# Two transformer blocks on one core: V as weights in two column groups, and scores from high and low parts, in three attentions

## The chip, the cores and the metric

The kernel runs on one core of a Trainium2 chip. The metric is the device time of one execution in microseconds. The work is issued by hand to the engines: TensorE (PE in the profile; its weight loads are PEld), VectorE (DVE), ScalarE (ACT), GpSimd (POOL) and SyncE (SP), which issues the DMA transfers. Each engine works through its own queue in order; semaphores order them among each other.

## The reference

Two blocks of two layers each, on 512 rows of x and 256 rows of context, width 1024, everything float32. The first block has a layer with two dense attentions side by side, then one with a windowed attention beside a short convolution:

```python
q, k, v, gate = heads(h @ w_in)            # norm, gain and rotation on q and k
kk, vv = concat(k_context, k), concat(v_context, v)
p = softmax(q @ kk.T * d ** -0.5)          # MLA: 8 heads, d = 96; GQA: 8 heads on 2 key heads, d = 64
o = p @ vv                                 # value width 64
mix = concat(o_mla, o_gqa) * silu(gate)
x = x + gate_of_modulation * (mix @ w_out) # the context rows too, with context keys alone
# second layer: 8 heads on 2 key heads, d = 64, a band of 3 blocks of 128 keys and the 256 context keys,
# softmax with one more logit per head (the sink)
```

The second block has three more attentions with values 128 wide, which the change leaves alone.

## The kernel before

Rows lie in tiles of 128: four of x (XT), two of context (CT). A projection is a chain of products whose float32 operands are split in a high part, rounded to fp32r, and a low part (the rest); three passes high x high, high x low and low x high give the product (L839 to L841). The five attentions share one function per engine, `attention(name)`: TensorE at L943, ScalarE at L1191, VectorE at L1514. The first three are "gqa", "mla" and "win". Their values are 64 wide; the heads are 64, 96 and 64.

A **unit** j is one head and one tile of 128 queries (`units_of`, L417). gqa and mla have 48 units: per head four x tiles with 768 keys (six blocks of 128) and two context tiles with 256 keys (two blocks), in the order 0, 4, 1, 5, 2, 3. win has 32: per head the tiles 0 to 3 with four, five, five and four blocks. All engines loop over j, and LAG = 1 (L429) staggers the steps. In iteration j they do, each in this order:

- TensorE: scores of unit j into a pair of PSUM banks (L994 and L995 for gqa, L997 for the others); turns (`prep`, L954) of q or k of the next head, from rows to columns, into bank 7; turns of the probabilities of unit j-1 (L1020) into banks 4 and 5; the product of the probabilities with V of unit j-2 (L1032) into bank 6, the turned probabilities as 128 x 128 weights and V as the 64 moving columns; then, in some iterations, a product of a modulation unit (L898, eight small products with 32 weight columns and 128 moving columns, in four column groups), its turn (L907), or a gate spread over all rows (L916).
- ScalarE: copies of the turned q or k (L1206; for gqa the high part, L1200); the exponential of unit j (L1226); the second part of the turned probabilities of unit j-1 (L1240); the copy of a modulation row (L1256).
- VectorE: a finished modulation column (L1463); the row maximum of unit j, as a minimum of negated scores (L1551, with a mask L1553; in win a second, tiny minimum with the sink, L1556); the low part of q or k, for gqa (L1525, L1529); the first part of the turned probabilities of unit j-1 (L1569); the reciprocal of the row sum and the final scaling of unit j-2 out of bank 6 (L1580, L1597), called "mixed". In gqa the steps of mla's norms follow at the end of the iteration (`mla_norms`, L1665), and in win those of the convolution.

The order around bank 6 is written out by hand: a PSUM bank notes who reads it last, and who writes it next waits for that. The product with V of unit i waits in this way for the final scaling of unit i-1:

```python
                        bank_free(6)                                   # the reader noted last
                        for n_, b in enumerate(bl):
                            mm = eng.matmul(psum[:, 6, 0:dv], prT[...], v_rows(name, h, b), ...)
                        mm.then_inc(*to("product_v", (name, i)))
                        reader[6] = ("mixed", (name, i))
```

`STACKED` (L506) names the attentions whose scores are formed from high and low parts stacked along the contraction: the 64 rows of q high lie over those of q low, and two passes against k high over k high and k low over k low give the product. Before, this is gqa alone; mla and win take their scores in full float32 from 96 and 64 rows (L997). The DMA loads are issued by SyncE in one queue: constants, modulation weights, then the weights of every stage in order, three buffers deep.

## Time and profile before

| | |
|---|---|
| Median of 3 runs | 1721.77 us (1720.62 to 1725.77) |
| The profiled execution | 1723.44 us, span 1721.6 us |
| TensorE busy | 1624.8 us (94% of the span) |
| TensorE weight loads | 1342.5 us (78%), beside the products |
| VectorE busy | 899.1 us (52%) |
| ScalarE busy | 647.5 us (38%) |
| GpSimd busy | 566.9 us (33%) |
| Mean granted TensorE clock | 0.971 of full speed |

The span is the time from the first to the last instruction. Busy time is the time in which an engine had an instruction under way; the ends of matmuls are modelled. The three attentions of the change lie at 246 to 401 us (gqa), 401 to 549 us (mla) and 792 to 892 us (win). A row of the timeline can merge several instructions of one form (the number behind x); a product in float32 counts twice there, one in fp32r and a turn once.

### The profile page before, as it was taken

The page shows a single profiled execution, that of the slowest core. Times are in us where ns is not written, and L with a number is a line of the kernel's source. Part 1 is how long each engine was busy: PE and PEld are TensorE (multiplying, and loading weights), DVE is VectorE, ACT ScalarE, POOL GpSimd, SP SyncE. Part 2 cuts the span into 40 slices and gives each one's busy share as a digit, 9 for nine tenths or more (in the row PEclk, how much of TensorE's full clock was granted, in tenths as well). Part 3 has the DMA queues.
Part 4 walks back from the last instruction along what each step waited for, and adds up shares of the span by engine and source line. Part 5 has one row for each costly group of instructions (what it writes and reads, how often), then busy time and mean ns, then how long its engine had stood idle before and what let it go on. Part 6 is the DMA issues. An engine that isn't in the chain of part 4 may idle for free.

```text
span 1721.6 us, 24787 instructions
## 1 busy us (share of the span) xinstructions
PE 1624.8 (94%) x9120; PEld 1342.5 (78%) x9120; DVE 899.1 (52%) x2120; ACT 647.5 (38%) x1320; POOL 566.9 (33%) x333
## 2 busy tenths in 40 slices
PE   4999889899999979999999999989999999999998
PEld 1788878797887858887888789956578778887787
DVE  2655737665554244924752688036531279916422
ACT  3322354354454323334542433344333343336322
POOL 1222231860001333446505344410424534431134
PEclk9999989899999989999999999969999999999999
DMA  8321212231013112331003232300112222220222
GB/s 326 83 73 46 62 50 87 71 90 50 26 38 111 62 31 80 93 97 57 1 1 101 86 98 83 90 0 1 50 49 86 95 86 98 98 74 1 80 92 86
DMA packets 93158, 124.40 MB, mean 72 GB/s; under 512 B 10288, under 2 KB 52208, under 8 KB 92016
## 3 DMA queue, kind: packets, MB, share of 16 engines
q1 hardware_dynamic: 93040, 122.82, 22.5%
q8 instruction: 75, 1.23, 0.3%
q14 instruction: 43, 0.35, 0.1%
HBM read 120.70 MB, written 2.10 MB: 71 GB/s over the span
## 4 chain that ended last, share of the span: by engine, by line
PE 86%; DVE 7%; ACT 3%; issue 2%; DMA 1%; POOL 1%; SPq 0%; DVEq 0%; ACTq 0%; POOLq 0%
PE psum L839 18%; PE psum L841 18%; PE psum L840 18%; PE psum L1032 10%; PE psum L997 8%; PE psum L1020 5%; PE psum L809 3%; PE psum L954 3%; DMA mod_w<-mod_w_in 1%; PE psum L994 1%; PE psum L898 1%; PE psum L999 1%; PE psum L995 1%; ACT rz L1188 1%; DVE row_rstd L1346 0%
## 5 line engine op out<-in xcount | busy, mean ns | idle before, releaser
L1757 POOL TENSOR_TENSOR wlo<-wraw,whi 128x1024 fp32r<-128x1024 f32 (+4 forms) x172 | 399.7, 2325 | 979.1 <-ACT whi L1083 979.0
L1083 ACT ACTIVATE whi<-wraw 128x1024 fp32r<-128x1024 f32 (+4 forms) x172 | 174.7, 1019 | 483.3 <-PE psum L841 483.3
L839 PE MATMUL psum<-whi,h2h 128*128 128x512 f32 (+2 forms) x800 | 309.3, 387 | 7.1 <-ACT buf L1132 5.9
L841 PE MATMUL psum<-whi,h2l 128*128 128x512 f32 (+2 forms) x800 | 305.8, 382 | 0.0
L840 PE MATMUL psum<-wlo,h2h 128*128 128x512 f32 (+2 forms) x800 | 305.5, 382 | 0.0
L839 PE MATMUL psum<-whi,hTh 128*128 128x512 f32 (+2 forms) x512 | 196.9, 385 | 9.5 <-DVE hTl L1454 7.3
L1226 ACT ACTIVATE pr<-psum,nmax 128x512 f32<-128x512 f32 (+1 forms) x208 | 137.9, 663 | 170.9 <-DVE nmax L1551 88.3
L841 PE MATMUL psum<-whi,hTl 128*128 128x512 f32 (+2 forms) x512 | 192.0, 375 | 0.0
L840 PE MATMUL psum<-wlo,hTh 128*128 128x512 f32 (+2 forms) x512 | 192.0, 375 | 0.0
L839 PEld LDWEIGHTS psum<-whi,h2h 128*128 128x128 f32 x800 | 150.7, 188 | 33.4 <-issue 8.0
L997 PE MATMUL psum<-kT,qT 64*128 64x256 f32 (+5 forms) x480 | 164.6, 452 | 7.1 <-DVE qT L1536 4.3
L841 PEld LDWEIGHTS psum<-whi,h2l 128*128 128x128 f32 x800 | 150.6, 188 | 26.6
L840 PEld LDWEIGHTS psum<-wlo,h2h 128*128 128x128 f32 x800 | 150.7, 188 | 25.3
L1020 PE MATMUL psum<-ident,pr 128*128 128x128 f32 x792 | 130.6, 286 | 9.2 <-ACT pr L1226 7.2
L1020 PEld LDWEIGHTS psum<-ident,pr 128*128 128x128 f32 x792 | 94.8, 146 | 34.8 <-ACT pr L1226 18.6
L839 PEld LDWEIGHTS psum<-whi,hTh 128*128 128x128 f32 x512 | 98.0, 191 | 25.3 <-issue 9.7
L841 PEld LDWEIGHTS psum<-whi,hTl 128*128 128x128 f32 x512 | 97.9, 191 | 17.0
L840 PEld LDWEIGHTS psum<-wlo,hTh 128*128 128x128 f32 x512 | 98.2, 192 | 15.2
L1551 DVE TENSOR_REDUCE nmax<-psum 128x1 f32<-128x768 f32 x96 | 74.9, 780 | 65.9 <-PE psum L997 41.4
L997 PEld LDWEIGHTS psum<-kT,qT 64*128 64x128 f32 (+2 forms) x480 | 79.9, 193 | 35.7 <-issue 19.0
L1569 DVE COPY prT<-psum 128x256 f32<-128x256 f32 (+1 forms) x208 | 90.6, 435 | 23.3 <-PE psum L1020 21.1
L1032 PE MATMUL psum<-gq,prT 128*128 128x64 f32 x736 | 93.7, 274 | 1.1 <-DVE rz L1597 1.1
(253 smaller groups left out, 2459.8 us busy)
## 6 DMA issues: line engine op xcount, KB each, us to landing
wraw<-mod_w_in SPq DMA_DIRECT2D x32, 512.0 KB, 3.8
wraw<-w_in_odd_in SPq DMA_DIRECT2D x32, 512.0 KB, 3.4
wraw<-cd_w_in_in SPq DMA_DIRECT2D x24, 512.0 KB, 3.6
wraw<-w_in_even_in SPq DMA_DIRECT2D x20, 512.0 KB, 3.9
mod_w<-mod_w_in SPq DMA_DIRECT2D x8, 1024.0 KB, 17.8
wraw<-ab_w_in_in SPq DMA_DIRECT2D x16, 512.0 KB, 3.6
wraw<-w_ple_gate_in SPq DMA_DIRECT2D x16, 512.0 KB, 3.9
wraw<-ab_w_out_in SPq DMA_DIRECT2D x8, 512.0 KB, 3.6
```

The lines of the kernel that those rows point to most:

```text
L809: mm = eng.transpose(psum[:, b, n_ * P:(n_ + 1) * P], turn[name]["rows"](t, k), ident[:, :])
L839: eng.matmul(dst, a[0], ww[0], start=first, stop=False)
L840: eng.matmul(dst, a[0], ww[1], start=False, stop=False)
L841: mm = eng.matmul(dst, a[1], ww[0], start=False, stop=last_)
L997: mm = eng.matmul(dst, q_, ks[0:dk, a:b], start=True, stop=name != "fox")
L1020: mm = eng.transpose(psum[:, bk, (b - b0) * P:(b - b0 + 1) * P], pr[:, i % 2, b * P:(b + 1) * P], ident[:, :])
L1032: mm = eng.matmul(psum[:, 6, 0:dv], prT[:, i % 2, n_ * P:(n_ + 1) * P], v_rows(name, h, b), start=n_ == 0, stop=n_ == len(bl) - 1)
L1083: eng.activation(whi[:, s, :, 0:w], wraw[:, u["id"] % RAW, :, 0:w], ACT.Copy).then_inc(*to("split_hi", u["id"]))
L1226: eng.activation(pr[:, j % 2, 0:w], psum_flat[:, s0 * 512:s0 * 512 + w], ACT.Exp, bias=nmax[:, j % 4:j % 4 + 1], scale=-1.0, accum_out=rsu ...
L1551: eng.tensor_reduce(m, sc, AX.X, ALU.min).then_inc(*(label or note("nmax", (name, j))))
L1569: eng.tensor_copy(prT[:, i % 2, 0:nb * P], psum[:, 4, 0:nb * P]).then_inc(*note("probs_a", (name, i)))
L1757: eng.tensor_tensor(wlo[:, s, :, 0:w], wraw[:, u["id"] % RAW, :, 0:w], f32(whi[:, s, :, 0:w]), ALU.subtract)\
```

## The change

For gqa, mla and win ("HALVED") the product with V changes sides: V (128 keys x 64) is the weights and the turned probabilities (128 keys x 128 queries) are the moving columns. The even blocks of keys go to the columns 0 to 63 of the array and so to PSUM partitions 0 to 63 of bank 6, the odd blocks to 64 to 127. ScalarE copies this 128 x 128 result to the tile o2, and one more product with o2 as weights and a constant of two stacked 64 x 64 identities as moving operand adds both halves and turns the result back, again into bank 6. On TensorE it stands in the iteration after the product with V, behind the scores and the turns of q and k. VectorE's final scaling waits for it and moves to the next iteration as well; each loop has one iteration more.

The scores of win are stacked as gqa's were. Those of mla ("PARTED", 96 rows don't stack) are formed in three fp32r passes: q high with k high, q high with k low, q low with k high. The high parts are copied out by ScalarE and the low parts computed by VectorE, now for all three. In win the separate minimum with the sink becomes the start value of the masked minimum. The constant is loaded behind `sel`, and some small tiles change place.

```diff
+    out["halves"] = np.concatenate([np.eye(64), np.eye(64)]).astype(np.float32)
...
-        STACKED = ("gqa",)
+        STACKED, PARTED = ("gqa", "win"), ("mla",)
+        ROUNDED = STACKED + PARTED
+        HALVED = ("gqa", "mla", "win")
...
         def parts_of(name, p_):
-            key, _, _, tiles, dst, _ = p_
+            key, _, _, tiles, dst, d = p_
+            if name in PARTED:
+                lo = (qTl if key[0] == "q" else kTl)[0:d, key[1] % 2, tiles[0] * P:(tiles[-1] + 1) * P]
+                return [dst], [lo]
...
+            load(halves[:, :], io["k_halves"], "load_sel", 1)
...
     (TensorE, attention)
-                for j in range(n_units + lag + 1):
+                for j in range(n_units + lag + 1 + int(name in HALVED)):
...
                             if name in STACKED:
                                 eng.matmul(dst, q_, ks[:, a:b], start=True, stop=False)
                                 mm = eng.matmul(dst, q_, kl[:, a:b], start=False, stop=True)
+                            elif name in PARTED:
+                                eng.matmul(dst, q_, ks[0:dk, a:b], start=True, stop=False)
+                                eng.matmul(dst, q_, kTl[0:dk, h % 2, a:b], start=False, stop=False)
+                                mm = eng.matmul(dst, qTl[0:dk, h % 2, t * P:(t + 1) * P], ks[0:dk, a:b], start=False, stop=True)
...
+                    if name in HALVED and lag + 1 < j:
+                        i = j - lag - 2
+                        eng.wait_ge(*at("o2_copied", (name, i)))
+                        eng.matmul(psum[:, 6, 0:dv], o2[:, i % 2, :], halves[:, :], start=True, stop=True)\
+                           .then_inc(*to("joined", (name, i)))
+                        reader[6] = ("mixed", (name, i))
...
                         bank_free(6)
                         for n_, b in enumerate(bl):
+                            if name in HALVED:
+                                c0 = 64 * (n_ % 2)
+                                mm = eng.matmul(psum[c0:c0 + 64, 6, 0:P], v_rows(name, h, b), prT[:, i % 2, n_ * P:(n_ + 1) * P],
+                                                start=n_ < 2, stop=n_ >= len(bl) - 2)
+                                continue
                             mm = eng.matmul(psum[:, 6, 0:dv], prT[:, i % 2, n_ * P:(n_ + 1) * P], v_rows(name, h, b),
                                             start=n_ == 0, stop=n_ == len(bl) - 1)
                         mm.then_inc(*to("product_v", (name, i)))
-                        reader[6] = ("mixed", (name, i))
+                        reader[6] = ("o2_copied" if name in HALVED else "mixed", (name, i))
...
     (ScalarE, attention, after the second copy of turned probabilities)
+                    if name in HALVED and lag < j:
+                        i = j - lag - 1
+                        eng.wait_ge(*at("product_v", (name, i)))
+                        eng.activation(o2[:, i % 2, :], psum[:, 6, 0:P], ACT.Copy).then_inc(*to("o2_copied", (name, i)))
...
     (VectorE, attention)
-                for j in range(len(units) + lag + 1):
+                later = int(name in HALVED)
+                for j in range(len(units) + lag + 1 + later):
...
-                            eng.tensor_tensor_reduce(sc, sc, bias, 1.0, 3.0e38, ALU.add, ALU.min, m).then_inc(*(label or note("nmax", (name, j))))
-                        if name == "win":
-                            after_last()
-                            eng.tensor_tensor(m, m, nsink[:, h:h + 1], ALU.min).then_inc(*note("nmax", (name, j)))
+                            most = nsink[:, h:h + 1] if name == "win" else 3.0e38
+                            eng.tensor_tensor_reduce(sc, sc, bias, 1.0, most, ALU.add, ALU.min, m).then_inc(*note("nmax", (name, j)))
...
-                    for p_ in preps.get(j, []) if name in STACKED else ():
+                    for p_ in preps.get(j, []) if name in ROUNDED else ():
                         low(p_)
...
-                    if lag < j:
-                        i = j - lag - 1
+                    if lag + later < j:
+                        i = j - lag - 1 - later
...
-                        eng.wait_ge(*at("product_v", (name, i)))
+                        eng.wait_ge(*at("joined" if later else "product_v", (name, i)))
```

## Rows read from the trace of the kernel before

**Rows 1.** The page, chain that ended last, by engine
```profile
PE 86%; DVE 7%; ACT 3%; issue 2%; DMA 1%; POOL 1%; SPq 0%; DVEq 0%; ACTq 0%; POOLq 0%
```

**Rows 2.** Busy by stretch (us): PE, PEld, DVE, ACT, POOL, clock, DMA, GB/s
```profile
246.50:400.90 154.40, 142.70 (x1316) 127.96 (x1316) 108.19 (x270) 66.84 (x170) 76.77 (x83) 0.93 0.29 83
401.00:549.00 148.00, 145.49 (x1104) 121.27 (x1104) 78.39 (x203) 72.75 (x174) 1.67 (x1) 1.00 0.16 51
792.00:892.00 100.00, 96.97 (x658) 83.00 (x658) 74.49 (x230) 53.98 (x147) 48.18 (x34) 1.00 0.03 12
```

**Rows 3.** Chain of waits: the same step of successive heads, gqa, then win
```profile
363.14 1.29 PE psum L1032 x12
...
379.31 1.29 PE psum L1032 x12
...
853.24 1.06 PE psum L1032 x10
...
864.68 1.06 PE psum L1032 x10
```

**Rows 4.** Timeline, mla: start, length in us, instruction, [idle before, releaser]
```profile
470.63 1.51 PE L997 MATMUL psum<-kT,qT 96*128 96x512 f32 x4
...
471.98 0.82 PE L1020 MATMUL psum<-ident,pr 128*128 128x128 f32 x6
...
472.18 0.96 DVE L1551 TENSOR_REDUCE nmax<-psum 128x1 f32<-128x768 f32 x1 [0.99 <-PE psum L997]
...
472.63 0.56 PE L1032 MATMUL psum<-cq,prT 128*128 128x64 f32 x4
...
473.05 0.55 DVE L1569 COPY prT<-psum 128x384 f32<-128x384 f32 x1
...
473.70 0.28 DVE L1597 SCALAR_TENSOR_TENSOR rz<-psum,rinv,rz 128x64 f32<-128x64 f32 x1
...
475.46 1.45 PE L1032 MATMUL psum<-cq,prT 128*128 128x64 f32 x12
...
476.84 0.64 PE L898 MATMUL psum<-wraw,silu_pad 128*32 128x128 f32 x16
...
477.42 0.70 PE L997 MATMUL psum<-kT,qT 96*128 96x256 f32 x2
```

**Rows 5.** Timeline, gqa, a low part, then a short and a long unit
```profile
363.14 0.68 DVE L1525 TENSOR_TENSOR qTs<-psum,qTs 64x512 fp32r<-64x512 f32 x1 [0.24 <-ACT qTs L1200]
...
370.80 0.38 PE L994 MATMUL psum<-kTs,qTs 128*128 128x256 f32 x1
...
371.34 0.42 DVE L1551 TENSOR_REDUCE nmax<-psum 128x1 f32<-128x256 f32 x1 [0.65 <-PE psum L995]
...
375.35 0.50 PE L994 MATMUL psum<-kTs,qTs 128*128 128x512 f32 x1
...
376.35 0.96 DVE L1551 TENSOR_REDUCE nmax<-psum 128x1 f32<-128x768 f32 x1 [1.12 <-PE psum L995]
```

**Rows 6.** Timeline, win
```profile
848.28 0.42 DVE L1569 COPY prT<-psum 128x256 f32<-128x256 f32 x1
...
848.60 1.35 PE L997 MATMUL psum<-kT,qT 64*128 64x256 f32 x6
...
849.01 0.28 DVE L1597 SCALAR_TENSOR_TENSOR rz<-psum,rinv,rz 128x64 f32<-128x64 f32 x1
...
849.88 0.77 PE L1020 MATMUL psum<-ident,pr 128*128 128x128 f32 x5
...
849.98 0.83 DVE L1553 CUSTOM_DVE_ANT_0 psum<-psum,bias_window 128x640 f32<-128x640 f32 x1 [0.69 <-PE psum L997]
```

**Rows 7.** Busy by stretch as in rows 2, two stretches of gqa
```profile
260.00:264.00 4.00, 2.45 (x21) 2.17 (x20) 3.65 (x8) 1.37 (x3) 1.83 (x2) 1.00 0.41 121
336.00:340.00 4.00, 4.00 (x19) 3.81 (x19) 1.76 (x5) 0.99 (x2) 3.84 (x3) 0.50 0.02 4
```

More of the change, by code:

```diff
@@ L148, in build @@
         ident = sb("ident", [P, P])
+        halves = sb("halves", [P, 64])
         bias_causal = sb("bias_causal", [P, 4 * P])
@@ L159, in build @@
         pos_f = sb("pos_f", [P, NX])
-        ang = sb("ang", [P, NX, 24])
-        turns = sb("turns", [P, NX, 24])
         cos2 = sb("cos2", [P, NX, 24])
@@ L187, in build @@
         fcum = sb("fcum", [P, NX, 4, 4])
+        ang, turns, mod_row = same_place([("ang", [P, NX, 24], F32), ("turns", [P, NX, 24], F32)], [("mod_row", [P, P], F32)])
         rx = sb("rx", [P, NT, D])
@@ L201, in build @@
         wlo = sb("wlo", [P, SPL, 2, CW], F32R)
-        qT1, kT1, pr1, prT1, qT2, kT2, pr2, prT2, fq, fk, qTs, kTs, mod_w6 = same_place(
-            [(n_, [P, 2, NT * P], F32) for n_ in ("qT1", "kT1", "pr1", "prT1")],
+        qTh, kTh, pr1, prT1, qT2, kT2, pr2, prT2, fq, fk, qTs, kTs, mod_w6 = same_place(
+            [("qTh", [P, 2, NT * P], F32R), ("kTh", [P, 2, NT * P], F32R)] + [(n_, [P, 2, NT * P], F32) for n_ in ("pr1", "prT1")],
             [(n_, [P, 2, NX * P], F32) for n_ in ("qT2", "kT2", "pr2", "prT2")] + [("fq", [2, 2, CW], F32), ("fk", [2, 2, CW], F32)],
@@ L511, in temps @@
                 return qTs, kTs, pr1, prT1
-            return (qT1, kT1, pr1, prT1) if name in ("gqa", "mla", "win") else (qT2, kT2, pr2, prT2)
+            return (qTh, kTh, pr1, prT1) if name in PARTED else (qT2, kT2, pr2, prT2)
         def keys_of(name, g):
@@ L573, in copied @@
         def copied(name, p_):
-            if name in STACKED:
+            if name in ROUNDED:
                 return ("heads_lo", (name, p_[0]))
@@ L970, in attention @@
                                 eng.wait_ge(*at(*copied(name, p_)))
-                                if name in STACKED:
-                                    eng.wait_ge(*at("heads_copied", (name, p_[0], int(p_[0][0] == "k"))))
+                                if name in ROUNDED:
+                                    eng.wait_ge(*at("heads_copied", (name, p_[0], int(name in STACKED and p_[0][0] == "k"))))
                         s0 = score_bank(j)
@@ L1022, in attention @@
                             reader[bk] = ("probs_a" if b0 == 0 else "probs_b", (name, i))
[L1023 removed]
+                    if lag < j <= n_units + lag:
                         i = j - lag - 1
@@ L1208, in attention @@
                 lag = LAG
-                for p_ in preps[-1] if name in STACKED else ():
+                for p_ in preps[-1] if name in ROUNDED else ():
                     prep(p_)
-                for j in range(len(units) + lag):
+                for j in range(len(units) + lag + int(name in HALVED)):
                     if (name, j - 1) in spread_at:
@@ L1231, in attention @@
                                            bias=nmax[:, j % 4:j % 4 + 1]).then_inc(*to("exp_sink", j))
-                    if j >= lag:
+                    if lag <= j < len(units) + lag:
                         i = j - lag
@@ L1529, in low @@
                         eng.tensor_copy(lows[1], f32(lows[0])).then_inc(*note("heads_lo", (name, p_[0])))
-                for p_ in preps[-1] if name in STACKED else ():
+                for p_ in preps[-1] if name in ROUNDED else ():
                     low(p_)
-                for p_ in preps[-1] if name not in STACKED else ():
+                for p_ in preps[-1] if name not in ROUNDED else ():
                     key, _, _, tiles, dst, d = p_
@@ L1548, in attention @@
                         bias = bias_of(name, t)
[L1549 removed]
                         if bias is None:
[L1551 removed]
+                            eng.tensor_reduce(m, sc, AX.X, ALU.min).then_inc(*note("nmax", (name, j)))
                         else:
[L1553 to L1556 removed]
+                            most = nsink[:, h:h + 1] if name == "win" else 3.0e38
+                            eng.tensor_tensor_reduce(sc, sc, bias, 1.0, most, ALU.add, ALU.min, m).then_inc(*note("nmax", (name, j)))
                     if name == "diff" and j in (5, 9):
                         (log_gates if j == 5 else running_sums)()
[L1559 removed]
+                    for p_ in preps.get(j, []) if name in ROUNDED else ():
                         low(p_)
```

16 lines of the change are left out of this document (7 added, 9 removed).

## The prediction

> **What bounds the kernel now.** I read the chain of waits first: TensorE carries 86% of it [rows 1]. The reader should see that almost any TensorE time saved counts, as long as TensorE stays the last to finish. So I cut the three changed stages out of the span. Before the change TensorE is busy 142.7 of 154.4 us in the first attention (gqa), 145.5 of 148 in the second (mla) and 97.0 of 100 in the windowed one (win); VectorE is busy 108, 78 and 74 us [rows 2]. That looks like room for VectorE. But busy time says nothing about order, so the timeline of single units comes next. A unit is one head and one tile of 128 queries. In mla (unit of 768 keys) the scores start at 470.63, the turns of the probabilities at 471.98, the product with V at 472.63: no gap on TensorE. VectorE works on the same scores meanwhile: row maximum at 472.18, copy of turned probabilities at 473.05, final scaling at 473.70 [rows 4]. The final scaling of unit j-2 frees bank 6 for the product of unit j-1, which is a whole iteration later. That slack is why TensorE never stands.
>
> Six units (one head) take 16.17 us in gqa and four units 11.44 us in win [rows 3]; in mla 148/8 = 18.5 us with its ends [rows 2].
>
> **What the change does to TensorE's own time.** All per unit of 768 keys unless said.
> - Product with V: six blocks take 1.38 us to the next instruction (475.46 to 476.84), 0.213 each plus 0.1 before an instruction in 32-column groups [rows 4]. With V as the weights each block moves 128 columns in 64-column groups. The nearest row is the modulation product, 128 columns in four 32-column groups: eight of them in 0.58 us (476.84 to 477.42) [rows 4]. 128 columns in four passes at 2.4 GHz are 0.213 us, shared by four groups 0.053, eight of them 0.43; the remaining 0.15 stands as idle behind them. With two groups I take 0.107 per block, 0.64 for six. Bounds: 0.053 (the rate of that row) and 0.213 (no overlap at all).
> - Change of column layout: the 0.1 before and the 0.15 behind of those two rows, 0.24 together per unit; bounds 0 and 0.4. So the new product is 0.88 us (0.45 for two blocks, 0.67 for four, 0.88 for five, where three rounds are needed).
> - The Trainium skill, page TensorEngine Tiling (Array Packing), section Key Properties, says that changing the tiling mode drains the engine. The trace agrees as far as the 0.15 us behind the modulation product goes. Without the drain the sum below would be about 25 us smaller.
> - The same skill, page TensorE: Matmul & The Clock Gate, Part 3, says weight loads overlap running matmuls only where the row groups differ; here they don't. By that rule a block stands at the upper bound or above, which is the last rival below. The modulation row speaks against it: its four groups also share all rows, and eight matmuls that would stream for 1.7 us in series are done in 0.58.
> - Joining product: 128 weights, 64 columns, one block at the old rate, 0.21 us.
> - Scores of gqa: unchanged. Two rounded passes of 768 columns reach VectorE's maximum 1.00 us after their start (375.35 to 376.35), 0.54 us for 256 columns (370.80 to 371.34) [rows 5]. mla goes from 1.55 (470.63 to 472.18, of which 0.20 is the way to VectorE) to three rounded passes: 1.00 plus one more pass of 0.32 is 1.32.
> - Scores of win: 640 columns in full precision with 64 rows take 1.28 us (848.60 to 849.88) [rows 6]. Stacked, two rounded passes take 0.55 for 512 columns and 0.65 for 640, plus 0.20 on the way. If the 128-column piece went at the full-precision rate it would be 0.3 more in half the units, 5 us in all.
>
> If TensorE alone counted, mla would gain (1.35-1.12) x 4 x 8 = 7 us and a little in its short units, win about 18 us, the product nearly nothing once join and layout are paid (1.28 - 0.88 - 0.21 = +0.19 in long units, 0.43 - 0.45 - 0.21 = -0.23 in those of two blocks). Some 30 us of 1723.
>
> **What the change does to the order.** This is the step that decides. The joining product of unit j-3 now runs on TensorE in iteration j, behind the scores of unit j. It writes bank 6. The next product with V (unit j-2, same iteration) writes bank 6 again and so waits for the final scaling of unit j-3. VectorE reaches that scaling in iteration j too, one iteration later than before, and behind three things of its own queue: the maximum of unit j (which waits for the scores just issued), the low parts of the next head's queries or keys, the copy of the probabilities of unit j-1. The slack of an iteration is gone and the iteration is a closed ring: scores, maximum, copy, scaling, product, scores. Behind the waiting product on TensorE stand the modulation products and the next scores, for which VectorE and ScalarE wait. The join and the turns (0.85 us) and ScalarE's copy of the halves (0.3) run beside VectorE's part and cost nothing; they would count only if the ring were shorter than TensorE's own time.
>
> The ring, from rows: maximum to copy 0.87 (472.18 to 473.05), copy to scaling 0.65, scaling 0.28 [rows 4]; for 256 keys the maximum is 0.42 long and holds the next for 0.35 [rows 5]. Hand-over to TensorE 0.05, an estimate (bounds 0 and 0.1).
> - gqa, per head (four long, two short units): scores with way and maximum 4 x (1.00+0.87) + 2 x (0.54+0.35) = 9.3; copy and scaling six times 0.93 less 0.3 for the short copies = 5.3; hand-over 0.3; product 4 x 0.88 + 2 x 0.45 = 4.4; three modulation products at 0.58 and their turns at about 0.2, 2.4; low parts of the queries, 0.68 for 512 columns [rows 5] and about 0.35 for 256, 1.0. Sum 22.7 against 16.17: +6.5 a head, +52 us.
> - mla: 4 x (1.32+0.87) + 2 x (0.65+0.35) = 10.8; 5.3; 0.3; 4.4; one modulation product and, in half the heads, a gate spread, 1.3; low parts of queries and of keys, 2.0. Sum 24.1, 193 us for eight with about 3 for the ends = 196 against 148: +48 us. The low parts are new here, and every one lies in the ring.
> - win, per head of four: scores with way 2 x 0.75 + 2 x 0.85 = 3.2; maximum 2 x 0.74 + 2 x 0.87 = 3.2 (0.83 for 640 columns [rows 6] and the read of its result; for 512 an estimate by columns; the separate minimum with the sink is gone); copy to end of scaling 848.28 to 849.29, 4 x 1.01 = 4.0 [rows 6]; hand-over 0.2; product 2 x 0.67 + 2 x 0.88 = 3.1; low part 0.7. Sum 14.4 against 11.44: +3.0 a head, +24 us.
>
> Together +124 us. The first high and low parts and one more iteration at the end of each stage add some 3 us that the next stage waits for; one 32 KB load at the start lies behind larger ones and is taken at nothing (cover: the transfers of the modulation weights that run there). The profiled execution has 1721.6 us of span and 1723.4 of time, 1.7 over the median shown. 1723.4 + 126 - 1.7 is about **1847 us**.
>
> **The rivals.**
> - TensorE's time decides (the other side): the ring closes in time because the scaling comes free before the join and the turns end. The point from which it decides is a VectorE part under 0.85 us behind the scores; the rows give 1.8 to 2.0. Then the 30 us of above come out: about 1692 us. For it: chain and busy shares of rows 1 and 2. Against it: the order of VectorE's queue. Chance 0.04.
> - The ring and TensorE's time balance out (a VectorE part near 1.1 us, or a product far cheaper than any row): 1720. Chance 0.03.
> - The clock joins in. TensorE would be busy some 60% of these stages, with a gap of over 1 us in each unit. Where it idled longer, in gqa, the granted clock fell to 0.50 for 336 to 340; in 260 to 264 it was busy 2.45 of 4 us and kept 1.00 [rows 7]. At 1.2 GHz scores and product double: about +1.3 us in a long unit of gqa, 1.7 in mla, 1.0 in win, 140 us if it held for all three stages. For a third of them +47: about 1894 us. For it: the gaps recur in every unit. Against it: the row with as large a gap and a full clock. Chance 0.18.
> - The column groups don't overlap (0.213 per block): +0.64 per long unit, some +65 us, 1912 us. For it: no row has 64-column groups. Against it: the modulation row. Chance 0.07. (This is where the rule of Part 3 on weight loads, in the Trainium skill, would lead.)
> - Forecast, ring with overlapping groups at full clock: the rest, 0.68. Its own range is 1815 (no layout cost, cheaper blocks) to 1885 (layout 0.4, small VectorE instructions held up as GpSimd works beside them).
>
> **The numbers.** The range reaches from the forecast's lower edge to the clock and overlap cases: 1812 to 1915. Slower by over 0.3% (about 5 us, what a measurement of this kernel can tell from no change): 0.93; within: 0.03; faster: 0.04.
>
> **What would show it.** In the changed profile TensorE stands over 1 us ahead of each product with V, released by VectorE's final scaling; its busy share in mla falls from 98% to 60 or 70%. A head of gqa takes near 22.7 us, of mla 24, of win 14.4. The product of six blocks takes 0.6 to 0.9 us to the next instruction, the joining one about 0.2, mla's scores of 768 keys 1.1. The final scaling starts right behind the copy without waiting for the join. All stages outside the three keep their times. The prediction is wrong if the product waits for nothing or for the turned probabilities, if heads take no longer than before, or, by its size, if the granted clock of these stages leaves 1.00.

## The result, and the profile after

The changed kernel takes **1902.32 us** (median of 4 runs, 1900.24 to 1909.86) against 1721.26 for the kernel before in the same comparison: a ratio of 1.1054, 95% interval 1.1018 to 1.1089. The profiled execution has a span of 1900.6 us and a mean granted clock of 0.937 (before 1721.6 and 0.971). The sign and the mechanism were right, and the time lies in the range (1812 to 1915); the point, 1847, was 55 us too low.

The page of the changed kernel: busy time of TensorE and VectorE, then the chain by engine (against [rows 1]).

```profile
PE 1647.2 (87%) x9456; PEld 1338.4 (70%) x9456; DVE 917.6 (48%) x2129; ACT 690.2 (36%) x1459; POOL 566.5 (30%) x333
...
PE 76%; DVE 11%; issue 6%; ACT 4%; DMA 1%; POOL 0%; SPq 0%; DVEq 0%; ACTq 0%
```

TensorE's busy time grew by 22 us, the span by 179. So 157 us of the loss are time in which TensorE stood. The chain says so too: TensorE's share fell from 86% to 76%, VectorE's rose from 7% to 11%, and "issue" from 2% to 6%. The same three stages as in [rows 2], in the changed kernel (columns as there: length, PE, PEld, DVE, ACT, POOL, granted clock, DMA share, GB/s):

```profile
242.90:452.60 209.70, 148.61 (x1406) 116.05 (x1406) 114.72 (x267) 82.35 (x219) 76.50 (x83) 0.88 0.21 61
468.90:674.10 205.20, 144.85 (x1228) 117.67 (x1227) 89.80 (x225) 82.12 (x211) 0.00 (x0) 0.93 0.11 34
927.90:1068.50 140.60, 99.50 (x726) 83.04 (x726) 67.60 (x208) 62.43 (x179) 42.44 (x32) 0.82 0.01 5
```

TensorE is busy about 70% of each stage. What it waits for is in the list of waits (who waited for whom: us in total, times, longest):

```profile
PE psum L1056 <- DVE rz L1626: 152.0, 125, 3.4
ACT o L1272 <- PE psum L1056: 124.3, 115, 2.4
```

L1056 is the product with V, L1626 VectorE's final scaling, L1272 ScalarE's copy of the halves. In 125 of 128 units the product waited for the scaling. One long unit of mla in the timeline shows the ring closed (start, length, instruction, idle before it and its releaser):

```profile
541.88 0.88 PE L1056 MATMUL psum<-prT,cq 128*64 128x128 f32 x12 [1.04 <-DVE rz L1626]
...
542.68 0.38 PE L918 MATMUL psum<-sel,mod_row 128*128 128x2 f32 x2
...
542.92 0.47 PE L1008 MATMUL psum<-kTh,qTh 96*128 96x512 f32 x1
...
544.26 0.96 DVE L1582 TENSOR_REDUCE nmax<-psum 128x1 f32<-128x768 f32 x1 [1.00 <-PE psum L1010]
...
544.50 0.33 PE L1029 MATMUL psum<-halves,o 128*128 128x64 f32 x2
...
544.70 0.59 ACT L1227 ACTIVATE qTh<-psum 96x512 fp32r<-96x512 f32 x1 [1.64 <-PE psum L965]
...
545.33 0.69 DVE L1556 TENSOR_TENSOR qTl<-psum,qTh 96x512 fp32r<-96x512 f32 x1
545.93 0.41 DVE L1598 COPY prT<-psum 128x256 f32<-128x256 f32 x1
...
546.45 0.28 DVE L1626 SCALAR_TENSOR_TENSOR rz<-psum,rinv,rz 128x64 f32<-128x64 f32 x1
...
546.88 0.88 PE L1056 MATMUL psum<-prT,cq 128*64 128x128 f32 x12 [1.82 <-DVE rz L1626]
```

From product to product it is 5.00 us: product 0.80, a modulation turn 0.24, scores to the maximum 1.34, maximum to low part 1.07, low part to copy 0.60, copy to scaling 0.52, scaling to product 0.43. The join, at 544.50, was long done.

One of e7's ten runs took 7522.9 us, and the ratio given for e7 leaves it out.

The table has the lengths of the stages in every kernel of this study, in us, read from the timelines: gqa from its first scores to its last product with V; "to mla" from there to mla's first product; mla from its first to its last product; "to win" on to win's first scores; win as gqa; the rest to the end of the span. The experiments are described below.

| kernel | median | gqa | to mla | mla | to win | win | rest |
|---|---|---|---|---|---|---|---|
| before | 1721.3 | 155.8 | 9.9 | 140.9 | 243.4 | 100.3 | 828.7 |
| after | 1902.3 | 209.6 | 16.3 | 205.3 | 253.8 | 140.6 | 832.1 |
| e1 scaling first | 1798.7 | 175.4 | 16.4 | 157.1 | 254.3 | 118.3 | 832.0 |
| e2 scores only | 1721.5 | 155.7 | 14.6 | 133.9 | 249.8 | 91.6 | 830.9 |
| e3 halves only | 1934.1 | 209.2 | 12.4 | 199.7 | 247.9 | 188.0 | 832.9 |
| e4 filled gap | 1889.4 | 204.8 | 16.5 | 197.8 | 254.6 | 135.7 | 831.8 |
| e5 no join | 1697.1 | 145.1 | 12.8 | 125.3 | 251.4 | 89.5 | 829.8 |
| e6 copy ahead | 1804.1 | 177.5 | 16.9 | 158.0 | 253.8 | 121.8 | 832.0 |
| e7 mla's scores only | 1718.6 | 155.0 | 14.6 | 133.9 | 244.4 | 98.4 | 827.8 |
| e8 as e6, win as before | 1772.9 | 176.1 | 17.8 | 158.0 | 248.4 | 98.4 | 830.0 |
| e9 join elsewhere | 1733.6 | 147.1 | 16.7 | 142.9 | 254.9 | 98.7 | 828.4 |
| e10 long units only | 1733.3 | 149.9 | 16.8 | 143.8 | 254.2 | 92.3 | 825.6 |
| e11 e9, split wait | 1715.7 | 146.7 | 14.7 | 133.4 | 253.6 | 93.9 | 829.4 |
| e12 halves in gqa alone | 1712.3 | 147.1 | 16.4 | 136.3 | 244.7 | 98.4 | 826.1 |

### The profile page after: what moved, and what is told of

It is laid out like the page before. It is cut to its first block, busy times and chain, and to the rows that moved or that the text cites. A ratio compares the mean times of both kernels' runs of the same rounds, so it can differ in the third digit from the quotient of the medians.

```text
span 1900.6 us, 25634 instructions
## 1 busy us (share of the span) xinstructions
PE 1647.2 (87%) x9456; PEld 1338.4 (70%) x9456; DVE 917.6 (48%) x2129; ACT 690.2 (36%) x1459; POOL 566.5 (30%) x333
## 4 chain that ended last, share of the span: by engine, by line
PE 76%; DVE 11%; issue 6%; ACT 4%; DMA 1%; POOL 0%; SPq 0%; DVEq 0%; ACTq 0%
PE psum L850 16%; PE psum L851 16%; PE psum L852 16%; PE psum L1056 5%; PE psum L1012 3%; PE psum L965 3%; DVE prT L1598 3%; PE psum L1059 3%; PE psum L820 2%; PE psum L1042 2%; PE psum L1005 2%; DVE rz L1626 2%; PE psum L1006 1%; PE psum L1008 1%; DMA mod_w<-mod_w_in 1%
## 5 line engine op out<-in xcount | busy, mean ns | idle before, releaser
L1056 PE MATMUL psum<-prT,gq 128*64 128x128 f32 x736 | 68.3, 311 | 93.7 <-DVE rz L1626 93.7
L1042 PE MATMUL psum<-ident,pr 128*128 128x128 f32 x792 | 140.6, 304 | 4.4 <-ACT pr L1253 3.2
L1056 PEld LDWEIGHTS psum<-prT,gq 128*64 128x64 f32 x736 | 48.6, 153 | 112.6 <-DVE prT L1598 109.1
L1042 PEld LDWEIGHTS psum<-ident,pr 128*128 128x128 f32 x792 | 107.6, 169 | 22.3 <-ACT pr L1253 12.9
L852 PEld LDWEIGHTS psum<-whi,hTl 128*128 128x128 f32 x512 | 98.7, 193 | 17.0
L1598 DVE COPY prT<-psum 128x256 f32<-128x256 f32 (+1 forms) x208 | 90.4, 435 | 26.7 <-PE psum L1042 24.6
L1056 PE MATMUL psum<-prT,cq 128*64 128x128 f32 x448 | 38.2, 299 | 58.2 <-DVE rz L1626 58.2
```

Source lines behind the costliest of these rows:

```text
L852: mm = eng.matmul(dst, a[1], ww[0], start=False, stop=last_)
L1042: mm = eng.transpose(psum[:, bk, (b - b0) * P:(b - b0 + 1) * P], pr[:, i % 2, b * P:(b + 1) * P], ident[:, :])
L1056: mm = eng.matmul(psum[c0:c0 + 64, 6, 0:P], v_rows(name, h, b), prT[:, i % 2, n_ * P:(n_ + 1) * P], start=n_ < 2, stop=n_ >= len(bl) - 2)
L1598: eng.tensor_copy(prT[:, i % 2, 0:nb * P], psum[:, 4, 0:nb * P]).then_inc(*note("probs_a", (name, i)))
```

## The experiments

The first four ask whether the ring, the scores, the new product or the clock carries the loss.

**e1, VectorE's final scaling ahead of its maximum, the join right behind the scores.**

```diff
     (TensorE: the join moves ahead of the turns of q and k)
     (VectorE, iteration j)
+                    if later:
+                        scale_out(j)          # reciprocal, wait for the join, final scaling of unit j-3
                     if j < len(units):
                         ... maximum of unit j
...
-                    if lag + later < j:
-                        ... final scaling of unit j-3, behind the copy
```

> Edit: VectorE does the final scaling of unit j-3 before the maximum of unit j, and the joining product stands right behind the scores. The ring theory (the product with V waits for a scaling that stands behind the maximum, the low parts and the copy) expects TensorE's 93.7 + 58.2 us of waits for the scaling to fall below 30 us and the time to 1750, between 1735 and 1790: not down to 1700, since the maximum now starts some 0.5 us later and ScalarE's exponential and copy of the halves follow it. The rate theory (the new products, the join and the changes of column layout are themselves what costs) expects over 1880, as all of them are still there.

Measured: 1798.73 us (1797.17 to 1800.5), ratio to before 1.0449 [1.0432, 1.0467]. The order of the two queues (VectorE's scaling, TensorE's join) is worth 104 us, with the same instructions. The product's wait for the scaling falls from 152 to 15 us, but the time ends 9 us above the range, for new waits came up:

```profile
DVE rz L1599 <- PE psum L1020: 147.6, 116, 2.4
...
PEld psum L1020 <- ACT o L1272: 65.0, 81, 2.3
```

L1020 is the join here. It now waits for ScalarE's copy of the halves, and VectorE, with the scaling at the head of its queue, waits for the join.

**e2, the scores only** (high and low parts for mla and win, product with V as before).

```diff
-        HALVED = ("gqa", "mla", "win")
+        HALVED = ()
```

> Edit: HALVED is empty, so only the scores of mla and win change. The ring theory expects TensorE to bound these stages as before and the shorter scores to count: 12 us less in mla, 15 in win, in all 1698, between 1688 and 1710. Its rival, that the new low parts on VectorE are what made mla slow, expects mla to take longer than its 148 us of before, and 1721 or more.

Measured: 1721.52 us (10 runs), ratio 1.0002 [0.9989, 1.0014]. A miss. The table says where it went: the stretch of mla's products is 7.0 us shorter, the 7 of the prediction (not the 12 expected here), win is 8.7 shorter and not 18 (here 15), and the stretches in front of mla, in front of win and behind win are 4.7, 6.4 and 2.2 longer. At win's start the granted clock fell as well (columns as in [rows 2]):

```profile
786.00:792.00 6.00, 4.41 (x25) 3.52 (x23) 0.00 (x0) 3.84 (x6) 1.02 (x1) 1.00 0.00 0
792.00:798.00 6.00, 0.98 (x4) 1.00 (x5) 4.10 (x5) 2.33 (x5) 5.90 (x4) 0.72 0.42 126
798.00:804.00 6.00, 6.00 (x42) 5.82 (x40) 3.39 (x7) 4.18 (x9) 5.64 (x5) 0.72 0.13 49
...
820.00:830.00 10.00, 9.75 (x81) 8.97 (x80) 9.18 (x24) 5.75 (x18) 9.39 (x8) 1.00 0.01 2
830.00:840.00 10.00, 8.08 (x64) 6.94 (x62) 8.66 (x27) 6.77 (x18) 9.47 (x8) 1.00 0.00 1
```

Win's first scores start at 797.0. Ahead of them TensorE stands 6.61 us, until ScalarE and VectorE have made the first high and low parts (before: 1.21 us, ahead of 792.56):

```profile
797.02 0.55 PE L1005 MATMUL psum<-kTs,qTs 128*128 128x256 f32 x1 [6.61 <-DVE qTs L1556]
```

From 820 to 830 VectorE, which also carries the convolution here, is busy 9.18 of 10 us, and from 830 to 840 TensorE only 8.08 (before: 10.00). That the shorter scores now run into VectorE fits these rows, but no run tests it. Behind 840 the granted clock was 0.93, where it was 1.00 before.

**e3, the halved product only** (mla's and win's scores in full precision).

```diff
-        STACKED, PARTED = ("gqa", "win"), ("mla",)
+        STACKED, PARTED = ("gqa",), ()
     (q, k of mla and win in float32 tiles of their own)
```

> Edit: scores of mla and win as before (full float32), the halved product with V in all three. The ring theory expects the ring to be longer by the longer scores and shorter by mla's low parts: 1890 to 1925. If the scores' part of the change carried a good share of the loss, the time is under 1860.

Measured: 1934.14 us (1933.13 to 1935.43), ratio 1.1232 [1.1216, 1.1249]. The halved product with its join carries all of the loss and more; next to it the new scores save 32 us. They save 47 in win (188.0 against 140.6) and lose some 15 in mla and ahead of mla and win. Win as a whole, in columns as in [rows 2]:

```profile
910.40:1098.40 188.00, 162.53 (x726) 119.38 (x726) 63.62 (x197) 61.58 (x178) 47.71 (x34) 0.56 0.02 6
```

The granted clock was 0.56 here, against 0.82 in the changed kernel. So the 47 us are not the price of longer scores alone: much of them is the clock, and the two are not separated. The value is 9 us above the range.

**e4, work in the gap**: in units of more than two blocks (the long ones of gqa and mla, all of win) three more joining products, into the same place, ahead of the waiting product with V.

```diff
+                    if name in HALVED and lag + 1 < j and fill(j):      # 3 in units of over two blocks, else 0
+                        i = j - lag - 2
+                        for n_ in range(fill(j)):
+                            mm = eng.matmul(psum[:, 6, 0:dv], o2[:, i % 2, :], halves[:, :], start=True, stop=True)
+                        mm.then_inc(*to("joined", (name, i)))
```

> Edit: the changed kernel with three more copies of the joining product behind the turns of each unit of more than two blocks, 0.64 us of matmuls in the gap before the product with V; the result is the same. If the granted clock that fell in these stages costs what is left between the ring at full clock (about 1850) and 1902, more matmuls in the gap keep it at 1.00 and the time falls by 20 to 50 us although work was added. If the clock costs little, the time stays at 1902 or rises by up to 15 us where the added products come to lie in the ring.

Measured: 1889.41 us (1884.22 to 1894.46), ratio 1.0972 [1.0943, 1.1002], granted clock 0.959 against 0.937 (gqa 0.93 against 0.88, mla 0.99 against 0.93, win 0.93 against 0.82). TensorE did more and the kernel was 13 us faster: the clock costs something. The gain is under the 20 to 50 expected; how much the added products, for whose last one the scaling waits, gave back was not separated.

The next four ask what the two column groups cost without the join, and whether the ring left in e1 can be opened.

**e5, no join.** The scaling reads the even half directly and goes back to its old iteration; the sum over the odd blocks is left out of the output.

```diff
-                    if name in HALVED and lag + 1 < j:
-                        ... joining product
-                        reader[6] = ("o2_copied" if name in HALVED else "mixed", (name, i))
+                        reader[6] = ("mixed", (name, i))
-                    ... ScalarE's copy to o2
-                later = int(name in HALVED)
+                later = 0
```

> The changed kernel without the join: no copy of the halves, no joining product, and VectorE's final scaling reads the even half of bank 6 directly, in the iteration and behind the product it had before the change (the sum over the odd blocks is left out of the output). The product with V in two column groups and the new scores stay. Ring theory (the join and the scaling it delays carry the whole loss): compared with the scores-only kernel at 1721.5 us, the product saves 1.38 - 0.84 = 0.54 us in each of 64 long units of gqa and mla, nothing in the short ones and nothing in win, where the units wait for VectorE and ScalarE: 1687 us, 1678 to 1705. No wait of the product for the scaling beyond some 0.1 us. Rival (the two column groups themselves, their change of layout or the clock they leave behind cost the time): over 1721 us.

Measured: 1697.07 us (1696.91 to 1700.77), ratio 0.9865 [0.985, 0.988], as the ring theory had it. The column groups themselves gain 24 us over e2. The product's groups and its waits (count, busy us, mean ns, idle before), first of this kernel:

```profile
L1049 PE MATMUL psum<-prT,gq 128*64 128x128 f32 x736 | 61.8, 291 | 1.2 <-DVE rz L1615 1.1
L1049 PE MATMUL psum<-prT,cq 128*64 128x128 f32 x448 | 35.0, 283 | 0.5 <-DVE rz L1615 0.5
```

and of the changed kernel:

```profile
L1056 PE MATMUL psum<-prT,gq 128*64 128x128 f32 x736 | 68.3, 311 | 93.7 <-DVE rz L1626 93.7
...
L1056 PE MATMUL psum<-prT,cq 128*64 128x128 f32 x448 | 38.2, 299 | 58.2 <-DVE rz L1626 58.2
```

The same products, with 1.7 us of idle time ahead of them in place of 152. The join, ScalarE's copy for it and the iteration it adds cost 205 us.

**e6, e1 with ScalarE's copy of the halves at the head of its next iteration.**

```diff
                 for j in range(len(units) + lag + 2 * int(name in HALVED)):
+                    if name in HALVED and lag + 1 < j:
+                        ... copy of the halves of unit j-3
...
-                    if name in HALVED and lag < j:
-                        ... copy of the halves of unit j-2, behind the second part of the probabilities
```

> The kernel with VectorE's scaling first and the join right behind the scores (1798.73 us), with ScalarE's copy of the halves moved from the end of its iteration to the start of the next, ahead of the exponential. That kernel still had 65 us of TensorE's join waiting for this copy and 148 us of VectorE's scaling waiting for the join. Theory: a second ring stood there (join, scaling, maximum, exponential, second part of the turned probabilities, copy of the halves, join) and is opened by the move; the copy then needs only the product, which ends before the scores. What is left between the end of the scores and the next product is join 0.2, hand-over 0.12, scaling 0.3, against 0.8 of turns: TensorE stands no more. Sum: the kernel without the join (1687) plus some 0.28 us of joining product in 128 units and a few waits: 1725 us, 1712 to 1755. Rival (VectorE's scaling ahead of the maximum delays the exponential and so the turns, whatever the copy does): 1775 to 1800 us, with TensorE's wait at the turns for the exponential.

Measured: 1804.09 us (1802.99 to 1805.65), ratio 1.0484 [1.0467, 1.0502]. A miss, and a badly chosen edit: between the end of one iteration and the head of the next hardly anything stands in ScalarE's queue, so the copy did not really move. The timeline shows the second ring whole:

```profile
508.09 0.96 DVE L1617 TENSOR_REDUCE nmax<-psum 128x1 f32<-128x768 f32 x1
...
509.09 0.90 ACT L1257 ACTIVATE pr<-psum,nmax 128x768 f32<-128x768 f32 x1 [1.97 <-DVE nmax L1617]
...
509.98 0.48 ACT L1271 ACTIVATE prT<-psum 128x384 f32<-128x384 f32 x1
510.35 0.28 ACT L1242 ACTIVATE o<-psum 128x128 f32<-128x128 f32 x1
...
510.68 0.43 PE L1020 MATMUL psum<-halves,o 128*128 128x64 f32 x2 [0.64 <-ACT o L1242]
...
511.22 0.28 DVE L1599 SCALAR_TENSOR_TENSOR rz<-psum,rinv,rz 128x64 f32<-128x64 f32 x1 [1.64 <-PE psum L1020]
...
511.61 0.96 DVE L1617 TENSOR_REDUCE nmax<-psum 128x1 f32<-128x768 f32 x1
```

Maximum, exponential, second part of the probabilities, copy of the halves, join, scaling, maximum: 3.52 us. As long as the scaling stands ahead of the maximum and the exponential ahead of the copy, it stays.

**e7, mla's three passes as the only change** (but win's minimum with the sink stays joined).

```diff
-        STACKED, PARTED = ("gqa", "win"), ("mla",)
+        STACKED, PARTED = ("gqa",), ("mla",)
-        HALVED = ("gqa", "mla", "win")
+        HALVED = ()
```

> The kernel before with mla's scores alone in three rounded passes (win's in full precision as before, product with V as before; win's minimum with the sink stays joined to the masked one). The scores-only kernel came to 1721.5 us where 1698 was expected. If win lost its gain at its start (first high and low parts with TensorE idle, then half clock) and in waits for VectorE and ScalarE, and mla lost a few us at its start, this one is 1717 us, 1711 to 1722. If mla's part is what cost (low parts in VectorE's queue), 1725 us or more.

Measured: median 1718.58 us of 10 runs, ratio 0.9982 [0.9973, 0.9992]. Within the range, and small: mla's 7.0 us less 4.7 at its start. Against e2, win is 6.8 longer, but the stretch ahead of it is 5.4 and the one behind it 3.1 shorter: the stacked scores of win earn nothing.

**e8, e6 with win as before the change.**

```diff
-        HALVED = ("gqa", "mla", "win")
+        HALVED = ("gqa", "mla")
     (and the scores as in e7)
```

> The kernel e6 with win as before the change (full-precision scores, old product, no join); gqa and mla with halves, join, VectorE's scaling first and the copy of the halves ahead. If TensorE's time decides in gqa and mla now, the gain there is (1.38 - 0.84 - 0.28) = 0.26 us in 64 long units less about 0.2 in 32 short ones, and 3 us from mla's scores: about 1710 us, 1700 to 1735, and 10 us or more under e6. If rings remain in gqa and mla it is above 1740 us.

Measured: 1772.94 us (1771.79 to 1774.68), ratio 1.0302 [1.0286, 1.0317]: 38 us above its range. The rings remain in gqa and mla, as the expectation's last sentence has it.

The last four keep the join and take it out of the ring.

**e9, the join behind the turns of the probabilities, into another bank**: the second of the pair of score banks that the unit just turned has left.

```diff
     (TensorE, behind the turns of unit j-1 and ahead of the product with V of unit j-2)
+                    if name in HALVED and lag + 1 < j:
+                        i, b5 = j - lag - 2, score_bank(j - 1) + 1
+                        bank_free(b5)
+                        eng.wait_ge(*at("o2_copied", (name, i)))
+                        eng.matmul(psum[:, b5, 0:dv], o2[:, i % 2, :], halves[:, :], start=True, stop=True)\
+                           .then_inc(*to("joined", (name, i)))
+                        reader[b5] = ("mixed", (name, i))
     (VectorE: maximum, low parts, scaling from that bank, copy)
```

> The changed kernel with the join kept but taken out of the ring: the joining product stands behind the turns of the probabilities and writes the second bank of the pair of score banks that the turned unit has just left, so that the product with V waits only for ScalarE's copy of the halves, an iteration old, and no longer for VectorE's scaling. The scaling reads that bank, behind the maximum and the low parts. Theory (the whole loss of 205 us against the kernel without the join, 1697 us, is the shared bank, and with it the order): the joining product now costs its own time, 0.2 to 0.25 us in 128 units, 26 to 32 us: 1725 us, 1712 to 1740. Waits of the product for the scaling: none. Rival (any join costs a wait of this size, since the scaling comes an iteration later wherever it is written): above 1780 us, as in the kernels with the scaling first, 1799 and 1804 us.

Measured: 1733.62 us (1731.86 to 1734.98), ratio 1.0072 [1.0056, 1.0088]. Of the join's 205 us this takes away 169, with the same instructions. Three things moved together: the join's bank, its place on TensorE, and VectorE's scaling, now ahead of the copy. What each is worth was not separated. The product waits for nothing (busy us, mean ns, idle before):

```profile
L1056 PE MATMUL psum<-prT,gq 128*64 128x128 f32 x736 | 60.8, 288 | 0.0
...
L1056 PE MATMUL psum<-prT,cq 128*64 128x128 f32 x448 | 35.1, 283 | 0.0
```

What is left shows at the scores (L1005 gqa and win, L1008 mla), whose second bank the scaling reads:

```profile
PE psum L1005 <- DVE rz L1599: 15.5, 27, 1.2
...
PE psum L1008 <- DVE rz L1599: 11.1, 26, 0.7
```

**e10, e9 with halves in the long units of gqa and mla alone**; their short units take the old product in the join's place, win the old product.

```diff
+                        if short(name, t):
+                            ... old product of unit j-3 into bank b5
+                        else:
                             ... join
```

> The kernel e9 with halves and join only in the units of 768 keys of gqa and mla; their units of 256 keys take the old product with V straight into the bank of the join, in its place; win keeps its stacked scores and takes the old product as before. Without the join gqa gained 10.7 us, mla 8.6 over its new scores, in 32 long units each (and lost or gained under 2 us in the short ones), so some 0.3 us a long unit; the join costs 0.2 to 0.25 of it. Sum: the scores-only kernel, 1721.5 us, less 0 to 0.1 us in 64 units: 1718 us, 1710 to 1726. If the moved scaling leaves a wait in the order, over 1735 us. If the halved product is worth its full 0.54 us a long unit once nothing waits, 1702 us.

Measured: 1733.29 us (1725.65 to 1734.0), ratio 1.006 [1.0044, 1.0077]. A miss (7 us above its range); the profiled execution was the fastest of six, 1725.65 us, so its rows do not explain the median. They show gqa 2.8 us longer than in e9. Why the move of the short product does not pay stays open.

**e11, e9 with the wait for the score banks split**: each is waited for at the first product that writes it.

```diff
-                        for b in range(s0, s0 + 2):
-                            bank_free(b)
-                            reader[b] = ("exps", (name, j))
+                        fresh = [s0, s0 + 1]
...
+                            b_ = s0 + c0 // 512
+                            if b_ in fresh:
+                                fresh.remove(b_)
+                                bank_free(b_)
+                                reader[b_] = ("exps", (name, j))
```

> The kernel with the join behind the turns (1733.6 us), and the scores wait for each of their two banks at the first product that writes it, not for both ahead of the first. That kernel had 15.5 us of gqa's and 11.1 us of mla's scores waiting for VectorE's scaling, which reads the second bank. If that wait is all that stood between TensorE's own time and the result: 1733.6 less up to 26 us, 1710 us, 1705 to 1722, under the kernel before (1721.8). If VectorE's scaling ends after the first bank's passes too, or the wait moves on to another, 1728 us or more.

Measured: 1715.74 us (1711.58 to 1720.61), ratio 0.9961 [0.9946, 0.9977]. With its whole computation, the join moved and the waits split, the kernel is 6 us faster than before. Against e9 mla gained 9.5 us, win 4.8. The join's 205 us are down to 19, about what 128 joining products of 0.17 us are (22 us, an estimate). The split wait was not tried on the kernel before.

**e12, e11 with halves in gqa alone, mla's new scores, win's old ones.**

```diff
-        HALVED = ("gqa", "mla", "win")
+        HALVED = ("gqa",)
     (and the scores as in e7)
```

> The kernel e11 with halves and join in gqa alone; mla in three rounded passes with the old product, win with the scores and the product it had before (its minimum with the sink joined to the masked one). From the lengths of the stages: gqa 155.8 us before, 147.1 with the join behind the turns, less most of its 15.5 us of waits; mla's three passes with the old product came to 1718.6 us in all with gqa as before. Sum: 1718.6 - 8.7 - up to 12 = 1703 us, 1698 to 1712. If gqa's gain is lost again at the start of mla: 1714 us or more.

Measured: 1712.31 us (1711.81 to 1714.05), ratio **0.9945** [0.9933, 0.9957], 0.3 us above its range and the fastest version of this study with the whole computation, 9.7 us under the kernel before. gqa is 7.9 us shorter than in e7.

## Why the prediction was right, and where its size was off

- **The ring: right.** The product waits for the scaling (152 us), e1 takes 104 us off by order alone, e5 removes the ring with the join, e9 removes it with the join kept.
- **The range: right by its width.** 1902 lies above the forecast's own range (1815 to 1885) and inside the stated one, which reaches up to the clock and overlap rivals. The clock brought a part of the missing 55 us, the overlap rival none; the rest came from terms that were priced too low, as follows. The prediction's own sign for a wrong size, that the granted clock leaves 1.00, came true (0.88, 0.93 and 0.82).
- **gqa: right in size, in part by luck.** Forecast +52 us, measured +53.8. A head at full clock took 23.9 us (294.34 to 318.25) where the sum gave 22.7; the hand-over accounts for 0.6 of the 1.2 (see mla). Eight such heads are 10 us more than summed, yet the stage is only 2 over the forecast, so something else in it came out 8 cheaper than the sum had it. It had stretches at half clock before too [rows 7]; the difference of 8 us fits their costing less after the change, but was not tested by itself.
- **mla: +64.4 where +48 was forecast.** Heads at full clock took 25.9 and 26.0 us (485.70 to 511.62, 537.67 to 563.65), not 24.1. Of the 1.9, 0.5 is no error: both carry a gate spread, of which the sum had half of one (four of the eight heads have one). 0.6 is the hand-over, 0.12 to 0.16 us six times and not 0.05. The rest stands in the short units, where VectorE comes to the low part before ScalarE has the high part:

```profile
548.34 0.42 DVE L1582 TENSOR_REDUCE nmax<-psum 128x1 f32<-128x256 f32 x1 [1.61 <-PE psum L1010]
...
548.57 0.38 ACT L1227 ACTIVATE qTh<-psum 96x256 fp32r<-96x256 f32 x1 [0.49 <-PE psum L965]
...
548.98 0.42 DVE L1556 TENSOR_TENSOR qTl<-psum,qTh 96x256 fp32r<-96x256 f32 x1 [0.21 <-ACT qTh L1227]
549.32 0.54 DVE L1598 COPY prT<-psum 128x384 f32<-128x384 f32 x1
```

  From the maximum to the low part it is 0.64 us here, in the sum 0.35: behind the maximum stands ScalarE's high part, and behind that TensorE's turns of q. 1.4 us in eight heads are 11 of the 16 us; the other 5 fit the stretches at half clock (below). "The join and the turns cost nothing" held: VectorE's copies waited 2.6 us for turns in all of mla, its scaling 2.5 for the join.
- **win: +40.3 where +24 was forecast. Here the clock did most of it.** At full clock the units follow the sum: from product to product 3.50 us, 3.20, and 4.48 with the queries' low part (1011.01 to 1015.49). With the fourth taken as 3.50, an estimate, a head is 14.7 (forecast 14.4). The first seven heads took 15.9 to 20.9, in the mean 17.5. Two products of four blocks and one of five at full clock, then one of five at the 1.2 GHz level:

```profile
1004.31 0.66 PE L1056 MATMUL psum<-prT,gq 128*64 128x128 f32 x8 [1.02 <-DVE rz L1626]
...
1007.81 0.66 PE L1056 MATMUL psum<-prT,gq 128*64 128x128 f32 x8 [1.23 <-DVE rz L1626]
...
1011.01 0.73 PE L1056 MATMUL psum<-prT,gq 128*64 128x128 f32 x9 [1.15 <-DVE rz L1626]
```

```profile
993.28 1.51 PE L1056 MATMUL psum<-prT,gq 128*64 128x128 f32 x10 [1.65 <-DVE rz L1626]
```

  At the lower level a unit takes 4.64 where it took 3.50 (1035.65 to 1040.29) and 4.22 where it took 3.20 (1040.29 to 1044.51), the 1.0 that the prediction gave for win. Adding up the excess of the units at a lowered clock gives some 12 us for the stage, an estimate. About 3 more lie in one unit of 6.39 us (986.89 to 993.28), in which the second key head is made ready. Its two low parts, with a copy behind each, lie in the ring, and TensorE's turns wait for the first:

```profile
989.31 0.68 DVE L1556 TENSOR_TENSOR kTs<-psum,kTs 64x512 fp32r<-64x512 f32 x1 [0.24 <-ACT kTs L1227]
990.03 0.42 DVE L1560 CAST kTs<-kTs 64x512 fp32r<-64x512 f32 x1
...
990.50 0.41 PE L965 MATMUL psum<-ident,gq 128*64 128x128 f32 x2 [1.85 <-DVE kTs L1560]
```

  The sums for gqa and win priced the queries' low parts alone and put those of the keys at nothing (in gqa the same wait, 1.85 us, stands at 338.00). The rival "the clock joins in" (chance 0.18, +47 us) was thus true in part: some 12 us in win and some 5 in mla, where the stretches 602 to 609 and 658 to 665 had 0.50 and 0.51. Ring and clock are no alternatives: with the ring opened the granted clock was 1.00 in mla and 0.94 in win (e11), against 0.93 and 0.82. The forecast should have added a part of that price.
- **The ends: +3 forecast, +20 measured. This is the term that was most undersized.** Ahead of mla 6.4 us, ahead of win 10.4, behind win 3.4. e7 and e2 put 4.7 of the first and 6.4 of the second on the first high and low parts, with TensorE idle.
- Sum of the differences: 2 in gqa, 16 in mla, 16 in win and 17 at the ends are 51 of the 53 us by which the span grew more than forecast.
- **The product: right.** Six blocks take 0.80 us to the next instruction, five 0.77 (1011.01 to 1011.78), four 0.59, two 0.36: 0.107 a block as taken, with 0.16 for the layout where 0.24 was. (By that 0.24 in 128 units the prediction's "about 25 us" without the drain would be 31.) The rule of the Trainium skill on the overlap of weight loads (TensorE: Matmul & The Clock Gate, Part 3) is not borne out for column groups: loads of 0.66 us for six blocks lay beside 0.88 us of product, and a block came out at half of 0.213. Nor do the busy shares of the kernel before bear it out: products 94% and loads 78% of one span must overlap. The rule of the Trainium skill on mode changes (TensorEngine Tiling (Array Packing), Key Properties) agrees with the 0.17 us of idle time behind each of these products.
- **TensorE's own gain of "some 30 us": too high.** The 30 had the join in, at 0.21 us in 128 units; without it the sum is some 57. e5, without the join, is 24.6 us under the kernel before, and e11, with it, 6.3. mla's scores gave their 7, less 4.7 at the start. Of win's 18 e2 shows 8.7, all of it lost again ahead of and behind the stage. So the rival "TensorE's time decides" (1692) would have been too fast even with the ring open: e11 came to 1716.

What stays open: e10's median, what each of e9's three moves is worth, why gqa's heads cost 10 us more and the stage only 2, and what decides when the granted clock falls.

## What to carry to other kernels

A step added between a product and the reader that frees its bank must be checked against the queue of that reader: here the join cost 205 us. Of these 169 came back when the same product was written to another bank, with its place and the reader's place in the queues moved as well, and 18 more when each bank was asked for only where it is written. Price a ring with its hand-overs and with the engine that feeds its steps (here the high part ahead of the low part), and if it leaves gaps on TensorE at each turn, add some of the half clock to the forecast instead of keeping it as a separate case. A stage that shortens its scores by high and low parts pays at its ends: here 4.7 of mla's 7.0 us, and all of win's 8.7.

## What the runs showed of the hardware

- Two column groups of 64 overlap: a block of 128 float32 columns took 0.107 us in the changed kernel (six blocks 0.80 us, two blocks 0.36, so 0.11 for each further one), about half of the 0.225 that 128 columns took in mla's full-precision scores before (768 columns in 1.35 us, 470.63 to 471.98 in [rows 4]).
- A rounded pass of 128 columns was not slower per column than one of 256: 0.06 us (1005.48 to 1005.54) against 0.12 (1005.24 to 1005.36).
- The granted clock does not follow busy time alone: in mla it stood at 1.00 from 469 to 567 with TensorE busy 4.1 to 5.6 of every 7 us, and at 0.50 from 602 to 609 behind a stretch of 5.18 busy of 7 at 0.86; in e4 more work in the gaps raised the mean from 0.937 to 0.959.
